# Latent stage in one block: norm, turn, queries, keys and values tile by tile, with all split weights on chip

## Chip, cores and metric

The kernel runs on one core of one Trainium2 chip. The metric is the time of one execution in microseconds (us), the median of several runs. A core has TensorE (PE), VectorE (DVE), ScalarE (ACT), GpSimd (POOL), and SyncE (SP), which here only issues transfers; sixteen DMA engines move data. Engines run their own instruction lists and meet through semaphores.

## What is computed

Two blocks of two layers each work on x, 1024 tokens by 1024. The change concerns the first layer of the second block, an attention over 1024 "latent" tokens whose keys and values come from the latents and from 256 context tokens:

```python
h  = modulate(rmsnorm_2(x, g_pre_mix[i]), shift_m, scale_m)
hc = modulate(rmsnorm_2(ctx, g_pre_mix[i]), cshift_m, cscale_m)
q, k, v = qkv_proj(h, w_qkv[j], g_q[j], g_k[j])      # 8 query heads, 2 key heads of 128
q = apply_axial_rope(q, cos, sin)
k = apply_axial_rope(k, cos, sin)
kc, vc = kv_proj(hc, w_qkv[j], g_k[j])               # context: keys and values only
k_all, v_all = concatenate([kc, k]), concatenate([vc, v])
y = latent_attention(q, k_all, v_all) @ w_o[j]
x = x + gate_m * rmsnorm_2(y, g_post_mix[i])
```

`w_qkv` is 1024 by 1536. Keys are normalised per head and multiplied by a gain; those of the latents are also rotated.

## The kernel before

Tokens stand in tiles of 128 on the partitions: 8 latent tiles in `X` and 2 context tiles. Each product is done three times, since both operands are split into a high part and what it leaves ("low"): high by high, high by low, low by high. The weights of `w_qkv` are three chunks of 512 columns (0 and 1 are queries, 2 is keys and values), each of 8 slices of 128 rows (`KT` is 8), so a tile's chunk takes 24 matmuls of 512 columns.

The stage runs in blocks one after another, and between two blocks all engines meet at a barrier:

1. `keep_rows` makes six row vectors for later stages and stores them.
2. `copies` loads the context rows; `gained` makes the pre-norm gains.
3. `turn` for the 2 context tiles: squares (ACT, L488), 1/sqrt (POOL), scaled rows (DVE, L511), eight PE transposes a tile (L615), columns times gain (DVE), plus shift (POOL), high part (ACT, L553), low part (DVE, L601).
4. `project` for chunk 2 of the context. POOL splits the weights slice by slice (high L243, low L246) into a ring of 4. The loop runs over chunks, slices and, innermost, tiles; each tile has its PSUM bank, and the banks are drained after each chunk by DVE (L402) and ACT (L417).
5. `gained`, `turn` and `project` again for the 8 latent tiles and all 3 chunks: 576 matmuls.
6. `copies` loads the rotation tables and the gains of queries and keys.
7. `heads` twice: norm, gain and rotation of the keys; then `turn_keys`: their transposes (PE L1388), high (ACT L1401) and low parts (DVE L1413).
8. `latent_attention`, then `turn` and `project` with `w_o`, as blocks of their own, and from there one long block that begins with `Residual`.

Queries go to `q_rows`, a second buffer of 32 KB a partition; `X` keeps the old rows, and `Residual` adds the two. Before the second mixer `X` had also been stored to DRAM as `x_kept`, and it is read back in `mixer_out`.

SP issues all transfers in one queue (q1).

## Time and profile before

| | |
|---|---|
| median of 3 runs (3928.38 to 3941.7) | 3938.45 us |
| the profiled execution | 3941.49 us |
| its span, first to last instruction | 3939.7 us |
| PE busy | 3501.0 us (89%) |
| DVE, ACT, POOL busy | 2223.2, 1653.0, 1414.8 us |
| mean granted TensorE clock | 0.931 |

The span is what the trace covers; some 1.8 us of the execution lie outside it. Of the clock, 1.00 is 2.4 GHz and 0.50 is 1.2 GHz. Times within the trace count from the first instruction. A row in order of time has the start, the duration, the engine, the line, what is written and read, and in brackets how long the engine had been idle and who released it. Matmul ends are modelled, so the distance between two starts says more than a duration.

### The profile page before, as it was taken

Reading aid. Unit: us, or ns where it says so; the run is one execution under the profiler, and the core shown is the slowest. Engines: PE = TensorE matmul, PEld = TensorE weight load, DVE = VectorE, ACT = ScalarE, POOL = GpSimd, SP = SyncE. Lnnn points to the kernel's source line nnn. Section 1 sums busy time; section 2 is a strip of 40 time slices with the busy share of each in tenths; the row PEclk is TensorE's granted clock in tenths of the full one; section 3 lists DMA queues with packets and bytes.
Section 4 is the critical chain, followed back from the end, with each engine's and each line's share of the span. In section 5 each row is a group of like instructions: output and inputs, shape, how many; then the busy total and the mean of one; then the engine's idle time right before and its main releaser. Section 6 shows DMA issues by size and latency. Waiting matters only on the chain. (4 is left out here: it accounts for less than half of the span.)

```text
span 3939.7 us, 60153 instructions
## 1 busy us (share of the span) xinstructions
PE 3501.0 (89%) x19010; PEld 3080.6 (78%) x19010; DVE 2223.2 (56%) x4510; ACT 1653.0 (42%) x3892; POOL 1414.8 (36%) x1824
## 2 busy tenths in 40 slices
PE   5999979999999997693999775999999959999998
PEld 4899767999999986582888654888787747888786
DVE  5466766555777773205777437656535556556434
ACT  1277411767777750102343133333324363333333
POOL 2365322555667753522111124444201214444000
PEclk8999979999999988796999887999999779999999
DMA  4311445111222231100000111222345212222354
GB/s 153 110 40 39 176 162 224 57 41 45 61 68 65 67 129 78 43 22 12 1 0 0 40 55 49 80 80 80 107 155 179 67 48 75 80 80 84 126 192 147
DMA packets 95294, 326.69 MB, mean 83 GB/s; under 512 B 10465, under 2 KB 37393, under 8 KB 82322
## 3 DMA queue, kind: packets, MB, share of 16 engines
q1 hardware_dynamic: 95122, 324.61, 23.4%
q8 instruction: 82, 1.34, 0.1%
q14 instruction: 90, 0.74, 0.1%
HBM read 267.66 MB, written 56.91 MB: 82 GB/s over the span
## 5 line engine op out<-in xcount | busy, mean ns | idle before, releaser
L363 PE MATMUL ps<-w_hi,hT_hi 128*128 128x512 f32 x848 | 338.4, 399 | 41.8 <-DVEq L379 25.6
L364 PE MATMUL ps<-w_lo,hT_hi 128*128 128x512 f32 x848 | 336.6, 397 | 0.0
L365 PE MATMUL ps<-w_hi,hT_lo 128*128 128x512 f32 x848 | 336.2, 396 | 0.0
L2098 PE MATMUL ps<-down_high,hidden_high 128*128 128x512 f32 x704 | 277.1, 394 | 15.6 <-DVE hidden_low L1999 15.2
L2081 PE MATMUL ps<-columns_combined,up_high_even 128*128 128x512 f32 x616 | 243.9, 396 | 46.9 <-POOL up_low_even L1866 32.7
L2100 PE MATMUL ps<-down_high,hidden_low 128*128 128x512 f32 x704 | 275.6, 391 | 0.0
L2099 PE MATMUL ps<-down_low,hidden_high 128*128 128x512 f32 x704 | 275.5, 391 | 0.0
L1997 DVE TENSOR_TENSOR down_low<-down_raw,down_high 128x1024 fp32r<-128x1024 f32 x88 | 107.8, 1225 | 272.8 <-ACT down_high L1914 272.8
L2082 PE MATMUL ps<-columns_combined,up_high_even 128*128 128x512 f32 x616 | 243.1, 395 | 0.0
L2083 PE MATMUL ps<-columns_combined,up_low_even 128*128 128x512 f32 x616 | 242.8, 394 | 0.0
L2081 PE MATMUL ps<-columns_combined,up_high_odd 128*128 128x512 f32 x616 | 239.6, 389 | 0.0
L2082 PE MATMUL ps<-columns_combined,up_high_odd 128*128 128x512 f32 x616 | 239.6, 389 | 0.0
L2083 PE MATMUL ps<-columns_combined,up_low_odd 128*128 128x512 f32 x616 | 239.6, 389 | 0.0
L1165 ACT ACTIVATE masked_then_probs<-masked_then_probs,unit_rows 128x256 f32<-128x256 f32 (+1 forms) x512 | 229.1, 451 | 3.2 <-DVE sink_term L1252 1.8
L363 PEld LDWEIGHTS ps<-w_hi,hT_hi 128*128 128x128 f32 x848 | 163.7, 193 | 79.1 <-POOL w_lo L246 13.8
L1914 ACT ACTIVATE down_high<-down_raw 128x1024 fp32r<-128x1024 f32 x88 | 93.1, 1058 | 269.9 <-PE ps L2100 255.5
L1047 PE MATMUL ps<-w_units,hT_hi 128*128 128x384 f32 (+1 forms) x512 | 184.9, 361 | 19.2 <-DVE w_units L1211 12.7
L1102 PEld LDWEIGHTS ps<-v_tiles,probsT 128*128 128x128 f32 x1600 | 200.1, 195 | 1.4 <-issue 1.4
L1049 PE MATMUL ps<-w_units,hT_lo 128*128 128x384 f32 (+1 forms) x576 | 199.4, 346 | 0.0
L1102 PE MATMUL ps<-v_tiles,probsT 128*128 128x64 f32 x1600 | 196.6, 274 | 0.8 <-DVE unit_rows L1325 0.8
L365 PEld LDWEIGHTS ps<-w_hi,hT_lo 128*128 128x128 f32 x848 | 163.2, 193 | 34.8
L364 PEld LDWEIGHTS ps<-w_lo,hT_hi 128*128 128x128 f32 x848 | 163.7, 193 | 34.1
(336 smaller groups left out, 9568.2 us busy)
## 6 DMA issues: line engine op xcount, KB each, us to landing
mod_weights<-in_w_mod SPq DMA_DIRECT2D x24, 2048.0 KB, 8.8
up_raw<-in_w_up SPq DMA_DIRECT2D x44, 1024.0 KB, 4.9
down_raw<-in_w_down SPq DMA_DIRECT2D x88, 512.0 KB, 3.6
hidden_columns<-hidden SPq DMA_DIRECT2D x44, 512.0 KB, 2.6
hidden_columns<-hidden_columns SPq DMA_DIRECT2D x88, 256.0 KB, 3.9
w_raw<-in_w_in_b SPq DMA_DIRECT2D x24, 768.0 KB, 4.5
group_rows<-unit_rows SPq DMA_DIRECT2D x64, 132.0 KB, 1.8
unit_rows<-group_rows SPq DMA_DIRECT2D x64, 132.0 KB, 2.1
```

The costliest lines, as they stand in the source:

```text
L363: nc.tensor.matmul(out, a, w_hi[:, s], start=(k == 0), stop=False)
L364: nc.tensor.matmul(out, a, w_lo[:, s], start=False, stop=False)
L365: last = nc.tensor.matmul(out, b, w_hi[:, s], start=False, stop=(k == KT - 1))
L1049: last = nc.tensor.matmul(zbank, lo, weights(w_hi, a.unit, k), start=False, stop=(k == KT - 1))
L1102: last = nc.tensor.matmul(o_bank[:, h * HD:(h + 1) * HD], pT[:, a.par, h, c], vs[:, tile], start=(c == a.slots[0]), stop=(c == a.slots[-1]))
L1165: act.activation(x, x, ACT.Exp, bias=own, scale=-1.0, accum_out=total).then_inc(core.probs.sem, 1)
L2081: nc.tensor.matmul(out, a_hi, combined.moving(0, z, k), start=(start and k == 0), stop=False, **again)
L2082: nc.tensor.matmul(out, a_hi, combined.moving(1, z, k), start=False, stop=False, **again)
L2083: last = nc.tensor.matmul(out, a_lo, combined.moving(0, z, k), start=False, stop=(k == 3), **again)
L2098: nc.tensor.matmul(out, h_hi[:, s, t], down_hi[:, s, cols], start=begin, stop=False)
L2099: nc.tensor.matmul(out, h_hi[:, s, t], down_lo[:, s, cols], start=False, stop=False)
L2100: last = nc.tensor.matmul(out, h_lo[:, s, t], down_hi[:, s, cols], start=False, stop=end)
```

## The change

Steps 1 to 7 become one block with one phase, `Latents`. It walks 13 slots (`SLOTS`). In slot i every engine does its part for several tiles at once: tile i is normalised and turned to columns, the products of tile i-1 are made, and the keys of tile i-1 are normalised and rotated; keys of tile i-3 are transposed and split. Tiles 0 and 1 are the context (chunk 2 alone), 2 to 9 the latents (chunks 2, 0, 1). All 24 weight slices are split once, high by ACT and low by DVE (chunk 2) or POOL (chunks 0, 1), and stay in SBUF (`qkv_high`, `qkv_low`); slices are loaded in pairs, 12 loads of 512 KB into two buffers, and slots 0 to 3 split four each of slices 8 to 23. The loop over slices is now inside the tile, so 24 matmuls in a row go to one bank. The shift is added where the columns leave PSUM, half by ACT and half by DVE. The row vectors are made in slots 1 and 2. Queries are written over the rows of `X`, which have been stored to `x_kept` (4096 KB) behind the fifth load of weights; `q_rows` is gone, and `Residual` loads the old rows from `x_kept` tile by tile. `heads`, `turn_keys` and `keep_rows` are gone; `latent_attention` itself is the same.

```diff
@@ -2121,12 +1987,13 @@
...
+        self.old = at("residual_old_rows", [P, TILES, D], F32, offset=top)
...
     def sync(self, sp):
         core = self.core
         sp.dma_start(self.factor[:], self.factor_row.partition_broadcast(P)).then_inc(core.post_row.sem, 16)
-        self.combined.load(sp, self.ahead.w_up, 0)
+        for m in range(TILES):
+            sp.dma_start(self.old[:, m], self.kept[:, m]).then_inc((core.ready0, core.ready1)[m % 2].sem, 16)
+            if m == 3:
+                self.combined.load(sp, self.ahead.w_up, 0)
+            if m % 2:
+                sp.wait_ge(core.ready0.sem, core.ready0.at(8 * m + 8))
+                sp.wait_ge(core.ready1.sem, core.ready1.at(8 * m + 8))
...
+                y, ready = X[:, m], (core.ready0, core.ready1)[m % 2]
                 dve.wait_ge(core.y_rstd.sem, core.y_rstd.at(m + 1))
                 dve.scalar_tensor_tensor(y, y, rs[:, 0, m:m + 1], self.factor[:], ALU.mult, ALU.mult).then_inc(core.y_scaled.sem, 1)
                 dve.wait_ge(core.y_scaled.sem, core.y_scaled.at(m + 1))
-                dve.tensor_tensor(X[:, m], X[:, m], y, ALU.add).then_inc(core.x_new.sem, 1)
+                dve.wait_ge(ready.sem, ready.at(8 * (m - m % 2) + 16))
+                dve.tensor_tensor(y, y, self.old[:, m], ALU.add).then_inc(core.x_new.sem, 1)
...
+class Latents:
...
+    SLOTS = ALL_TILES + 3
...
+        self.w_hi = core.sb(st, "qkv_high", [P, 3, KT, 512], F32R)
+        self.w_lo = core.sb(st, "qkv_low", [P, 3, KT, 512], F32R)
+        self.raw = core.sb(st, "qkv_raw", [P, 2, 2, 512])
+        self.T_hi = core.sb(st, "columns_high", [P, 2, KT, P], F32R)
+        self.T_lo = core.sb(st, "columns_low", [P, 2, KT, P], F32R)
...
+    def sync(self, sp):
+        core = self.core
+        sp.dma_start(self.C[:], self.ctx_rows).then_inc(core.loads.sem, 16)
+        def load(p):
+            c, k = self.slice_at(2 * p)
+            sp.dma_start(self.raw[:, p % 2], self.w[c][:, k:k + 2]).then_inc((core.raw0, core.raw1)[p % 2].sem, 16)
+        load(0)
+        load(1)
...
+        for p in range(2, 3 * KT // 2):
+            if p < 2 + KT // 2:
+                sp.wait_ge(core.split.sem, core.split.at(2 * p - 2))
+            else:
+                sp.wait_ge(core.up_lo.sem, core.up_lo.at(2 * p - 2 - KT))
+            load(p)
+            if p == 4:
+                sp.dma_start(self.kept, self.X[:]).then_inc(core.x_kept.sem, 16)
+        sp.wait_ge(core.links_act.sem, core.links_act.at(1))
+        sp.dma_start(self.lines_dram.rearrange("n (k p) -> (n k) p", p=P), self.lines[:]).then_inc(core.row_vectors.sem, 16)
+        sp.wait_ge(core.row_vectors.sem, core.row_vectors.at(16))
...
+    def gpsimd(self, pool):
...
+        def low(n):
+            c, k = self.slice_at(n)
+            pool.wait_ge(core.high.sem, core.high.at(n + 1))
+            pool.nop(nofuse=True)
...
+        for i in range(self.SLOTS):
+            t = self.tile(i + 1)
+            if t is not None:
+                rstd(t)
+            if i < 4:
+                for n in range(KT + 4 * i, KT + 4 * i + 4):
+                    low(n)
...
+    def scalar(self, act):
...
+        def high(n):
+            c, k = self.slice_at(n)
+            if n % 2 == 0:
+                raw = (core.raw0, core.raw1)[(n // 2) % 2]
+                act.wait_ge(raw.sem, raw.at(16 * (n // 4) + 16))
+            act.activation(self.w_hi[:, c, k], self.raw[:, (n // 2) % 2, n % 2], ACT.Copy).then_inc(core.high.sem, 1)
+        square(0)
+        for n in range(4):
+            high(n)
+        square(1)
+        for i in range(self.SLOTS):
+            t = self.tile(i + 1)
...
+                square(t)
+            t = self.tile(i)
+            if t is not None:
...
+                for k in range(4):
+                    act.activation(self.tmp[:, k], ps[:, 0, k * P:(k + 1) * P], ACT.Identity, scale=self.pre[:, self.of(t), k:k + 1],
+                                   bias=self.shifts[self.of(t)][:, k:k + 1]).then_inc(core.n_columns.sem, 1)
+                act.wait_ge(core.n_columns.sem, core.n_columns.at(4 * t + 4))
+                act.wait_ge(core.n_columns_dve.sem, core.n_columns_dve.at(4 * t + 4))
+                if t >= 2:
+                    act.wait_ge(core.products.sem, core.products.at(t - 1))
+                    if t >= 2 + CTX_TILES:
+                        act.wait_ge(core.val.sem, core.val.at(t - 1 - CTX_TILES))
+                act.activation(self.T_hi[:, t % 2], self.tmp[:], ACT.Copy).then_inc(core.hi_done.sem, 1)
...
+            if i < 4:
+                for n in range(KT + 4 * i, KT + 4 * i + 4):
+                    high(n)
+            t = self.tile(i - 1)
+            if t is not None:
+                act.wait_ge(core.products.sem, core.products.at(t + 1))
+                if t >= 2:
+                    act.wait_ge(core.kq_turned.sem, core.kq_turned.at(t - 1))
+                act.activation(self.k_rows[:, t % 2], ps[:, 4 + t % 2, 0:KV2 * HD2], ACT.Copy).then_inc(core.parts_act.sem, 1)
+                act.activation(self.v[:, t], ps[:, 4 + t % 2, KV2 * HD2:], ACT.Copy).then_inc(core.parts_act.sem, 1)
+                act.wait_ge(core.parts_act.sem, core.parts_act.at(2 * t + 1))
...
+                act.activation(self.k_sq[:], self.k_rows[:, t % 2], ACT.Square).then_inc(core.sq.sem, 1)
...
+                    act.wait_ge(core.val.sem, core.val.at(m + 1))
+                    if m == 0:
+                        act.wait_ge(core.x_kept.sem, core.x_kept.at(16))
+                    act.activation(self.X[:, m, 512:D], ps[:, 7, :], ACT.Copy).then_inc(core.acc_used_act.sem, 1)
...
+                act.wait_ge(core.kq_turned.sem, core.kq_turned.at(t + 1))
+                act.activation(self.kT_hi[:, :, t * P:(t + 1) * P], ps[:, 2 + t % 2, 0:KV2 * P].rearrange("p (g t) -> p g t", t=P), ACT.Copy)\
+                   .then_inc(core.kq_hi.sem, 1)
...
+    def vector(self, dve):
...
+                if t + 1 < ALL_TILES:
+                    normed(t + 1)
+                dve.wait_ge(core.hi_done.sem, core.hi_done.at(t + 1))
+                dve.tensor_tensor(self.T_lo[:, t % 2], self.tmp[:], self.T_hi[:, t % 2].bitcast(F32), ALU.subtract).then_inc(core.lo_done.sem, 1)
...
+            t = self.tile(i - 1)
+            if t is not None:
+                k3 = self.k_rows[:, t % 2].rearrange("p (h d) -> p h d", d=HD2)
+                sq3 = self.k_sq[:].rearrange("p (h d) -> p h d", d=HD2)
+                dve.wait_ge(core.sq.sem, core.sq.at(t + 1))
+                dve.reduce_sum(self.ksum[:, t], sq3, axis=AX_X).then_inc(core.sums.sem, 1)
+                if t >= CTX_TILES:
...
+                        dve.wait_ge(core.x_kept.sem, core.x_kept.at(16))
+                    dve.tensor_copy(self.X[:, m, 0:512], ps[:, 6, :]).then_inc(core.acc_used_dve.sem, 1)
+                dve.wait_ge(core.rstd.sem, core.rstd.at(t + 1))
...
+    def tensor(self, pe):
...
+        def product(t, c, bank, done):
+            for k in range(KT):
...
+                a, b = self.T_hi[:, t % 2, k], self.T_lo[:, t % 2, k]
+                nc.tensor.matmul(ps[:, bank, :], a, self.w_hi[:, c, k], start=(k == 0), stop=False)
+                nc.tensor.matmul(ps[:, bank, :], a, self.w_lo[:, c, k], start=False, stop=False)
+                last = nc.tensor.matmul(ps[:, bank, :], b, self.w_hi[:, c, k], start=False, stop=(k == KT - 1))
+            last.then_inc(done.sem, 1)
+        for i in range(self.SLOTS):
...
+                for k in range(KT):
+                    last = nc.tensor.transpose(ps[:, k // 4, (k % 4) * P:(k % 4 + 1) * P], self.nrows[:, k * P:(k + 1) * P], core.ident[:])
+                last.then_inc(core.n_turned.sem, 1)
+            t = self.tile(i - 1)
+            if t is not None:
+                pe.wait_ge(core.lo_done.sem, core.lo_done.at(t + 1))
+                if t >= 2:
+                    pe.wait_ge(core.parts_act.sem, core.parts_act.at(2 * t - 2))
+                product(t, 2, 4 + t % 2, core.products)
+                if t >= CTX_TILES:
+                    m = t - CTX_TILES
+                    if m >= 1:
+                        pe.wait_ge(core.acc_used_dve.sem, core.acc_used_dve.at(m))
+                    product(t, 0, 6, core.gate)
+                    if m >= 1:
+                        pe.wait_ge(core.acc_used_act.sem, core.acc_used_act.at(m))
+                    product(t, 1, 7, core.val)
...
+                for g in range(KV2):
+                    last = nc.tensor.transpose(ps[:, 2 + t % 2, g * P:(g + 1) * P], self.k_rows[:, t % 2, g * HD2:(g + 1) * HD2], core.ident[:])
+                last.then_inc(core.kq_turned.sem, 1)
...
-        keep_rows()
...
-                T = split_columns(st2)
...
-                    C = q_rows[:, 0:CTX_TILES]
-                    copies(core, [(C, I["ctx"][0].rearrange("(m p) n -> p m n", p=P))])
...
-                    turn(core, CTX_TILES, Stage(core, x_rows(C)), T, scale=pre[:], shift=mod_ctx[:, 0:8],
-                         ahead=weights)
-                    project(core, T, plain_tokens, CTX_TILES, weights, 1, lambda m, c: kv_rows[:, m])
-                gained(core, pre[:], vcol("g_pre_mix"), mod[0][:, 8:16])
-                weights = Weights(core, st2, I["w_qkv"])
-                turn(core, TILES, Stage(core, x_rows(X)), T, scale=pre[:], shift=mod[0][:, 0:8], ahead=weights)
-                project(core, T, plain_tokens, TILES, weights, 3, lambda m, c: (
-                    kv_rows[:, CTX_TILES + m] if isinstance(c, int) else q_rows[:, m, bass.ds(c * 512, 512)]))
+                latents = Latents(core, st2, X, x_dram, I["ctx"][0].rearrange("(m p) n -> p m n", p=P), I["w_qkv"], I["gain_k2"], tables,
+                                  I["axial"], (kT_hi, kT_lo), v, RowVectors(core, vcol, mod, pre_ffn), rows_dram,
+                                  (mod_ctx[:, 8:16], mod[0][:, 8:16]), (mod_ctx[:, 0:8], mod[0][:, 0:8]))
+                in_one_block(core, [latents])
...
-                copies(core, [(tables[:], I["axial"]), (gain_q[:], I["gain_q2"].partition_broadcast(P)),
-                              (gain_k[:], I["gain_k2"].partition_broadcast(P))])
...
-                heads(core, CTX_TILES, keys, KV2, HD2, gain_k[:])
-                heads(core, TILES, lambda m: keys(m + CTX_TILES), KV2, HD2, gain_k[:], rotated)
-                turn_keys(core, keys, kT_hi, kT_lo)
-                latent_attention(core, tile_part(q_rows)(0, D), gain_q[:], tables, kT_hi, kT_lo, kv_rows[:, :, KV2 * HD2:], top)
...
+                copies(core, [(gain_q[:], I["gain_q2"].partition_broadcast(P))])
+                latent_attention(core, tile_part(X)(0, D), gain_q[:], tables, kT_hi, kT_lo, v)
+        with ExitStack() as st:
+            T = split_columns(st)
+            weights = Weights(core, st, I["w_o"])
+            turn(core, TILES, Rows(core, tile_part(X)(0, D)), T, ahead=weights)
+            project(core, T, plain_tokens, TILES, weights, 2, lambda m, c: X[:, m, bass.ds(c * 512, 512)])
```

Three places in the order of instructions. First the transfers that SP issues. Before, from the row vectors to the last load ahead of attention (`w_raw` are the weights, `q_rows` holds the context rows here):

```order
L3133 DMA row_vectors<-row_lines 48x128 [waits links_dve]
L3106 UNCONDITIONAL_BRANCH [waits row_vectors]
L2403 UNCONDITIONAL_BRANCH [waits barrier_Pool_Activation_PE_DVE_SP_release]
L2406 DMA q_rows<-in_ctx 128x2x1024
L2402 UNCONDITIONAL_BRANCH [waits loads]
L619 UNCONDITIONAL_BRANCH [waits barrier_Pool_Activation_PE_DVE_SP_release]
L233 DMA w_raw<-in_w_qkv 128x2048 x2
```

Now, the whole block and the load ahead of attention:

```order
L2459 DMA context_rows<-in_ctx 128x2x1024
L2463 DMA qkv_raw<-in_w_qkv 128x1024 x2
L2466 DMA gain_keys<-in_gain_k 128x256
L2467 DMA axial<-in_axial 128x1024
L2463 DMA qkv_raw<-in_w_qkv 128x1024 [waits split] x3
L2475 DMA x_kept<-x 128x8192
L2463 DMA qkv_raw<-in_w_qkv 128x1024 [waits split]
L2463 DMA qkv_raw<-in_w_qkv 128x1024 [waits up_lo] x6
L2477 DMA row_vectors<-row_lines 48x128 [waits links_act]
L3210 UNCONDITIONAL_BRANCH [waits row_vectors]
L2278 UNCONDITIONAL_BRANCH [waits barrier_Pool_Activation_PE_DVE_SP_release]
L2281 DMA gain_queries<-in_gain_q 128x1024
```

The store of `x` has moved between the fifth and the sixth load of weights, and each later load waits until a buffer has been split.

Second, ScalarE. Before, in the turn of the latent tiles it did nothing but squares and high parts:

```order
L488 ACTIVATE squares,sum_sq<-q_rows 128x1024 [waits rstd] x2
L553 ACTIVATE hT_hi<-columns 128x8x128 [waits shifted] x2
L544 REGISTER_ALU
L544 COMPARE_AND_BRANCH
L533 UNCONDITIONAL_BRANCH
```

Now, from slice 8 in slot 0 to the columns of tile 1 in slot 1 (`qkv_raw` are the loaded slices):

```order
L2540 ACTIVATE qkv_high<-qkv_raw 128x512 [waits raw0]
L2540 ACTIVATE qkv_high<-qkv_raw 128x512
L2540 ACTIVATE qkv_high<-qkv_raw 128x512 [waits raw1]
L2540 ACTIVATE qkv_high<-qkv_raw 128x512
L2531 ACTIVATE squares,statistics<-x 128x1024 [waits y_squared]
L2533 ACTIVATE statistics<-statistics,eps 128x1 [waits y_squared]
L2557 ACTIVATE columns<-ps,modulation_ctx,pre_gains 128x128 [waits lo_done,n_turned]
```

The splits of weights stand in ScalarE's list ahead of the columns of the next tile, and wait there for their loads.

Third, TensorE. Before, the transposes of the keys stood in a block of their own, behind all products:

```order
L365 MATMUL ps<-w_hi,hT_lo 128x512
L299 UNCONDITIONAL_BRANCH
L1380 UNCONDITIONAL_BRANCH [waits barrier_Pool_Activation_PE_DVE_SP_release]
L1382 UNCONDITIONAL_BRANCH
L1382 ISA
L1386 REGISTER_ALU [waits staged]
L1388 MATMUL ps<-identity,key_rows 128x128 [waits lo_done]
```

Now, from the end of slot 3 to the first product of slot 4 (`normed_rows` is the next tile):

```order
L2691 MATMUL ps<-qkv_high,columns_low 128x512
L2732 MATMUL ps<-identity,key_rows 128x128 [waits staged]
L2732 MATMUL ps<-identity,key_rows 128x128
L2700 MATMUL ps<-identity,normed_rows 128x128 [waits n_columns_dve,n_columns,n_rows]
L2700 MATMUL ps<-identity,normed_rows 128x128 x7
L2689 MATMUL ps<-qkv_high,columns_high 128x512 [waits parts_act,lo_done]
L2690 MATMUL ps<-qkv_low,columns_high 128x512
```

Key transposes and the turn of the next tile now stand between the products of two tiles.

## Rows read from the trace of the kernel before

**Rows 1.** Busy time by stretch: PE, PEld, DVE, ACT, POOL, then PEclk, DMA, GB/s.

```profile
1541.00:1571.00 30.00, 4.13 (x18) 3.47 (x18) 8.98 (x22) 4.30 (x6) 14.54 (x14) 0.56 0.30 106
...
1584.00:1637.00 53.00, 14.46 (x65) 12.99 (x64) 28.95 (x35) 17.48 (x25) 36.33 (x32) 0.64 0.11 40
1637.00:1771.00 134.00, 133.34 (x576) 110.03 (x576) 8.03 (x12) 6.58 (x11) 37.99 (x40) 0.98 0.09 32
1771.00:1830.00 59.00, 5.78 (x22) 3.52 (x20) 25.05 (x65) 11.98 (x31) 20.32 (x44) 0.52 0.06 20
```

**Rows 2.** VectorE in order of time: stage start, first drain of two chunks.

```profile
1540.88 0.17 DVE L3109 TENSOR_TENSOR row_columns<-vectors,modulation 128x8 f32<-128x8 f32 x1 [0.31 <-PEq L299]
...
1679.58 0.69 DVE L402 COPY q_rows<-ps 128x512 f32 x1 [44.02 <-PE ps L365]
...
1723.09 0.69 DVE L402 COPY q_rows<-ps 128x512 f32 x1 [38.75 <-PE ps L365]
```

**Rows 3.** ScalarE in order of time: last drain, after the loads, latent attention, residual.

```profile
1771.26 0.60 ACT L417 ACTIVATE kv_rows<-ps 128x512 f32<-128x512 f32 x1 [0.76 <-PE ps L365]
1777.94 0.72 ACT L682 ACTIVATE head_squares<-kv_rows 128x256 f32<-128x256 f32 x2 [6.08 <-DVEq L711]
...
1830.31 1.06 ACT L1590 ACTIVATE query_squares<-q_rows 128x1024 f32<-128x1024 f32 x1 [0.89 <-PEq L1379]
...
2341.48 1.49 ACT L2210 ACTIVATE residual_columns_even<-ps,modulation,pre_gain_ffn 128x128 f32<-128x128 f32 x4
```

**Rows 4.** TensorE in order of time: products after idling, and ten transposes.

```profile
1571.51 0.63 PE L364 MATMUL ps<-w_lo,hT_hi 128*128 128x512 f32 x1
1571.94 0.63 PE L365 MATMUL ps<-w_hi,hT_lo 128*128 128x512 f32 x1
...
1576.43 0.39 PE L363 MATMUL ps<-w_hi,hT_hi 128*128 128x512 f32 x1
1576.66 0.39 PE L364 MATMUL ps<-w_lo,hT_hi 128*128 128x512 f32 x1
...
1855.54 1.25 PE L1509 MATMUL ps<-identity,probs 128*128 128x128 f32 x10
```

**Rows 5.** DMA issues between 1454.5 and 1456 us: KB each, us to landing.

```profile
x<-x_kept SPq DMA_DIRECT2D x1, 4096.0 KB, 14.0
w_raw<-in_w_out_b SPq DMA_DIRECT2D x1, 1024.0 KB, 16.0
```

**Rows 6.** DMA issues of the whole page, KB each, median us to landing.

```profile
down_raw<-in_w_down SPq DMA_DIRECT2D x88, 512.0 KB, 3.6
...
w_raw<-in_w_qkv SPq DMA_DIRECT2D x8, 1024.0 KB, 4.9
```

**Rows 7.** Groups by line, 1540 to 1831 us: busy, mean ns, idle before.

```profile
L246 POOL TENSOR_TENSOR w_lo<-w_raw,w_hi 128x512 fp32r<-128x512 f32 x27 | 34.7, 1286 | 4.2 <-POOL w_hi L243 0.4
...
L553 ACT ACTIVATE hT_hi<-columns 128x1024 f32 (+1 forms) x10 | 10.6, 1057 | 37.9 <-POOL columns L567 37.9
...
L488 ACT ACTIVATE squares<-x 128x1024 f32 x8 | 8.3, 1043 | 1.2 <-PEq L2521 1.2
...
L511 DVE TENSOR_SCALAR rows<-x,rstd 128x1024 f32 x8 | 6.0, 754 | 11.9 <-POOL rstd L503 11.9
...
L682 ACT ACTIVATE head_squares<-kv_rows 128x256 f32 (+1 forms) x10 | 3.9, 413 | 32.1 <-DVE kv_rows L727 21.7 <-DVEq L711 10.4
```

**Rows 8.** VectorE in order of time, 2400 to 2412 us: the same subtraction twice.

```profile
2401.80 2.72 DVE L1738 TENSOR_TENSOR residual_columns_odd<-residual_columns_odd 128x512 f32<-128x512 f32 x1
...
2411.20 0.69 DVE L1744 TENSOR_TENSOR residual_columns_odd<-residual_columns_odd 128x512 f32<-128x512 f32 x1
```

**Rows 9.** GpSimd in order of time, the same stretch.

```profile
2401.40 2.58 POOL L1866 TENSOR_TENSOR up_low_even<-up_raw,up_high_even 128x1024 fp32r<-128x1024 f32 x1 [2.45 <-ACT up_high_even L1901]
```

**Rows 10.** The chain that ended last, start of the residual phase.

```profile
2325.88 4.29 DMA residual_factor<-row_vectors
...
2331.52 1.24 DVE x L2266
```

385 lines of the change are left out of this document (213 added, 172 removed).

## The prediction, made before the changed kernel had run

> **What bounds the stage now.** I read the busy time by stretch first, since the totals of the page mix stages. The stage begins with VectorE's first row vector at 1540.9 us [rows 2] and ends where latent attention begins on ScalarE, at 1830.3 [rows 3]: 289.4 us. Only one of its stretches is full. From 1637 to 1771 TensorE is busy 133.3 of 134 us, at a granted clock of 0.98 [rows 1]. Everywhere else it mostly waits: in 1541 to 1571 it works 4.1 us of 30, in the turn of the latent tiles (1584 to 1637) 14.5 of 53, while the keys are finished (1771 to 1830) 5.8 of 59 [rows 1]. So some 155 us of the stage hold next to no products, and the reader is to see that no other engine fills them either: they are chains through several engines with barriers between. What the change can give is at most what lies outside the products.
>
> **The floor.** VectorE drains the first two chunks 43.4 us apart (1679.58 and 1723.09) [rows 2]. That is 192 matmuls, 0.2264 us each, as the distance between two starts at full clock shows too (0.23) [rows 4]. The same matmuls stay: 48 for the context and 576 for the latents, 141.3 us. Transposes cost 0.115 us each at full clock (ten take 1.25 with the tail of the last) [rows 4], so a tile's eight take about 1.0.
>
> **A full slot (tiles 3 to 9).** Eight transposes 1.0, 72 matmuls 16.3, two key transposes 0.3, hand-overs 0.1: 17.7 us. Does TensorE wait within it? ScalarE may take the keys of tile i-1 only when the key transposes at the end of slot i are done (the buffer `k_rows` has two places), so its work bunches behind each slot. From there to a free bank for chunk 0: ScalarE's two copies and a square of 256 columns, 0.41 each [rows 7], a VectorE sum of about the same, VectorE's drain 0.69 [rows 2], with hand-overs about 3 us. TensorE meanwhile has 1.0 of transposes and 5.4 of chunk 2. The columns of the next tile follow: its square 1.04 [rows 7], the mean, four columns 1.49 [rows 3], high part 1.06 [rows 7], low part 1.3 to 1.6, in all about 8 us after the slot's end, and needed only after 17.7. Nothing waits. What hides the keys is thus the 16.3 us of products; without it they would cost what they cost now, most of the 59 us from 1771 on [rows 1] over ten tiles, 5 us a tile.
>
> **The ramp (slots 0 to 3).** Zero is the block's start. The context rows are issued at 0.3 and land in 4.9, as the other 1024 KB load does [rows 6]. Square, 1/sqrt, scaling (0.75) [rows 7], eight transposes at half clock (TensorE has idled; 2 us), ScalarE's first four splits and second square, columns, high and low part: the first low part is done at about 15.7, and the context product of tile 0 fits between 16 and 24. The loads of slices 4 to 7, 3.6 us each [rows 6], arrive at 13 to 15. The fifth load waits for six low parts, which VectorE has at 17.3; the store of `x` (4096 KB) goes out right behind it at 17.8, and the sixth load at 18.8. In the trace a 4096 KB transfer lands in 14.0, and a 1024 KB load issued just behind it in 16.0 [rows 5], where one alone takes 4.9 [rows 6]: one queue, served in order. The sixth load is half that size, so I take 15.2: it lands at 34. ScalarE stands at slice 10 until then, with the square of tile 2 and the columns of tile 1 behind it in its list.
>
> After 34: two splits 1.2 (about 0.6 for 512 columns, half of the 1.06 for 1024), square and mean 1.5, columns 1.5, high 1.1, low 1.3, and 0.4 of hand-overs: the product of tile 1 starts at 41. It runs at half clock for its first 4 us (starts 0.43 apart) and then at full clock (0.23) [rows 4]: 7.4 us, to 49. The low parts of slices 12 to 15 keep GpSimd until 46 (1.29 each) [rows 7]; only then does it make the 1/sqrt for the keys of tile 0, and VectorE has that ahead of tile 2's columns. So tile 2 is ready at 52. From there TensorE is not idle again: chunks 2, 0 and 1 of tile 2 take 16.3 us, to 68.4. Slices 20 to 23 are loaded by 60, high by 63 and low by 66.5; chunk 1 wants its last slice at 67.7. That is close, 1.2 us.
>
> **One correction to the ramp.** GpSimd's subtractions run beside VectorE's here. VectorE's subtraction of two 512-column operands takes 0.69 us alone and 2.72 [rows 8] where GpSimd has a 2.58 us subtraction under way [rows 9]: VectorE waits for that operation to end. In slots 1 to 3 eleven small operations for the row vectors and about six larger ones meet sixteen such GpSimd operations of 1.29. If each of the seven small two-operand ones waited once, that is 9 us; if none did, nothing. I take 1.5, near the lower end, since VectorE has no other work until GpSimd is through at 46. The Trainium skill, "SBUF — State Buffer", section "Who interferes with whom", says the same of the pair of ports that the two engines share: an exclusive lock for the whole instruction. By that rule, if all seven meetings lay on the path, the sum would be 3862; it is the part of the skill that speaks against this change.
>
> **Sum.** Slot 3 ends at 68.4 + 0.3 + 1.5 = 70.2. Seven full slots add 123.9: 194.1. The tail (last drain, two rounds of key transposes, high and low parts) is 3.5, the barrier 0.3: 198. The block that loads the query gain stays: from the last drain to the next ScalarE work it takes 6.1 us with three loads now (1771.9 to 1777.9) [rows 3], and 5.3 with one. The stage lasts 203.2 us in place of 289.4, a gain of 86.2.
>
> **Residual.** VectorE added the first row of y at 2331.5, 5.6 us after the factor was issued at 2325.9 [rows 10]. Now the old row (512 KB) comes behind the factor (512 KB) in the queue. The two are as large as one 1024 KB load, 4.9 us [rows 6], which with two issues and a hand-over is 5.6, the moment of today's addition; two separate loads of 3.6 in a row would be 7.9. I take 1.1 us later, nearer to the first; the chain of the phase starts with that addition, so it is lost in full (bounds 0 and 2.5). The later rows are issued in pairs well before their turn. `latent_attention` and the `w_o` stage do the same work as now, on other addresses: 0. They start at half clock as now, since TensorE idles in front of them either way.
>
> 3941.5 - 86.2 + 1.1 = 3856 for the profiled execution, which is 3 us above the median of the three runs; against that median the forecast is 3854.
>
> **Rivals.**
> 1. The store of `x` does not hold up the sixth load. Against it stand the 16.0 us [rows 5]. For it: that load was behind a read, this one is behind a write. The sixth load would then land at 24 and not at 34, less what the buffers then cost: 3845.
> 2. The weights set the pace of the ramp: the loads take longer than 3.6 us beside each other, or the lock above costs more. Each of six loads from the seventh on can add 1 to 2 us once chunk 1's 1.2 us of slack is used: 3862 to 3870.
> 3. The full slots are longer, because the bunched work of ScalarE and VectorE takes more than the 6.4 us that I give it before chunk 0. At 3 us a slot that is 21: 3875. For it: every hand-over in the list of ScalarE is in order and I counted 0.1 each. Against it: the margin is twice the chain. In this case too the key work is not hidden, and the change does only half of what it says.
> 4. Slower than before: TensorE is granted half clock in the full slots. With starts 0.43 apart [rows 4], a slot is 33 us; from six of eight such slots on the change loses, and with all eight the time is 3854 + 8 x 15.5 = 3978. Against it: the clock is 0.98 over 134 us of the same products [rows 1]; for it only that in each slot the engine does short transposes and waits on more semaphores.
>
> **Chances.** Forecast 0.62, rival 1 0.12, rival 2 0.15, rival 3 0.08, rival 4 0.02, and 0.01 for no net change from several small causes. The range 3838 to 3872 takes in the forecast with an error of some 10 us in a ramp worked out, rival 1 and rival 2, and leaves out rivals 3 and 4. A measurement of this kernel tells a change from none at about 0.3%, 12 us. Faster by more than that 0.97, within it 0.01, slower 0.02.
>
> **What would show it.** In the trace after: one stretch of some 140 us with TensorE over 97% busy and a clock near 1.00; full slots 17.7 us apart (look at the first transpose of each tile); ScalarE idle for more than 10 us in slot 0, released by a transfer into `qkv_raw`; tile 2's first product 52 to 54 us after the block's start; latent attention beginning 203 us after it; in the residual phase a first addition released by `residual_old_rows`. The forecast is wrong if a slot is longer than 18.5 us, if chunk 1 of tile 2 waits for `qkv_low` for several us, if the ScalarE wait is missing, or if attention itself takes another time.

## The result

| | before | after |
|---|---|---|
| median of the runs, us | 3939.6 (3928.4 to 3941.7, 4 runs) | 3849.4 (3843.0 to 3852.0, 4 runs) |
| ratio, 95% interval | | 0.9774 (0.9752 to 0.9796) |
| profiled execution: span | 3939.7 | 3848.0 |
| latent stage, block start to latent attention | 289.4 | 201.5 |

The forecast was 3854, range 3838 to 3872. The two spans differ by 91.7 us. Along the trace this is made up of: a stage that starts 1.0 earlier (same code ahead of it), the stage itself 87.9, latent attention and the `w_o` stage 0.1 (495.6 us from the first query square to the issue of the residual factor before, 495.5 after), the residual phase -0.2 (from that issue to the first store of hidden columns 114.0 before, 114.2 after), and 2.8 in the unchanged rest. The thirteen profiles of this study, the kernel before among them, ran that rest in 1492 to 1500 us, so the 2.8 can't be told from chance.

Busy time by stretch of the changed kernel, with the columns of [rows 1]: ramp to the sixth weight load, tile 1, tile 2, the seven full slots, the tail with the block that loads the query gain.

```profile
1539.80:1571.00 31.20, 11.04 (x40) 8.64 (x40) 10.59 (x23) 11.02 (x22) 3.60 (x4) 0.62 0.82 305
1571.00:1588.60 17.60, 10.46 (x41) 8.33 (x41) 11.55 (x23) 12.89 (x28) 10.39 (x11) 0.69 0.30 94
1588.60:1608.20 19.60, 19.47 (x74) 15.78 (x75) 4.71 (x11) 7.61 (x17) 11.83 (x11) 0.84 0.18 56
1608.20:1729.70 121.50, 121.50 (x571) 101.25 (x568) 40.85 (x91) 33.44 (x80) 19.07 (x40) 1.00 0.00 1
1729.70:1741.30 11.60, 0.86 (x4) 0.29 (x2) 4.00 (x10) 2.38 (x7) 2.34 (x5) 0.72 0.14 45
```

TensorE is busy through all of the fourth stretch, at full clock. The keys' 59 us of [rows 1] have shrunk to the last row. Of what TensorE waits for in the stage, the view of waits leaves three lines:

```profile
PE ps L2700 <- DVE normed_rows L2607: 27.2, 4, 14.3
PE ps L2732 <- DVE kT_lo L2676: 5.5, 1, 5.5
PE ps L2689 <- DVE columns_low L2636: 0.6, 1, 0.6
```

ScalarE in order of time: the splits of slices 8 and 10, the high part of tile 2, a key copy behind each of slots 3 and 4 and behind the last full one, the start of latent attention.

```profile
1560.02 1.15 ACT L2540 ACTIVATE qkv_high<-qkv_raw 128x512 fp32r<-128x512 f32 x2 [3.76 <-DMA qkv_raw<-in_w_qkv]
1570.95 1.15 ACT L2540 ACTIVATE qkv_high<-qkv_raw 128x512 fp32r<-128x512 f32 x2 [9.79 <-DMA qkv_raw<-in_w_qkv]
...
1586.36 1.06 ACT L2565 ACTIVATE columns_high<-columns 128x1024 fp32r<-128x1024 f32 x1 [3.62 <-issue]
...
1608.52 0.38 ACT L2577 ACTIVATE key_rows<-ps 128x256 f32<-128x256 f32 x1 [8.44 <-PE ps L2732]
...
1626.24 0.38 ACT L2577 ACTIVATE key_rows<-ps 128x256 f32<-128x256 f32 x1 [9.70 <-PE ps L2732]
...
1729.78 0.38 ACT L2577 ACTIVATE key_rows<-ps 128x256 f32<-128x256 f32 x1 [14.86 <-PE ps L2732]
...
1741.33 1.06 ACT L1456 ACTIVATE query_squares<-x 128x1024 f32<-128x1024 f32 x1 [4.89 <-PEq L2277]
```

The second row is the wait behind the store of `x`. In a full slot ScalarE idles 9.4 to 9.7 us, for the key transposes: that is the spare time which the products leave it.

VectorE in slot 1: a normalised tile, the row vectors, the sum for the keys of tile 0, their scaling, and only then tile 2's columns.

```profile
1574.76 0.75 DVE L2607 TENSOR_SCALAR normed_rows<-x,statistics 128x1024 f32<-128x1024 f32 x1 [16.41 <-POOL statistics L2486]
...
1577.13 1.23 DVE L2758 TENSOR_TENSOR row_columns<-vectors,modulation 128x8 f32<-128x8 f32 x1
...
1582.46 0.41 DVE L2650 TENSOR_REDUCE statistics<-key_squares 128x2 f32<-128x256 f32 x1
1584.11 0.43 DVE L2658 TENSOR_TENSOR key_squares<-key_rows,statistics 128x256 f32<-128x256 f32 x1 [1.24 <-POOL statistics L2509]
...
1584.92 1.36 DVE L2631 TENSOR_SCALAR columns<-ps,pre_gains,modulation 128x128 f32<-128x128 f32 x4
```

GpSimd over the same time, four weight subtractions in one row, and the first step of the keys' 1/sqrt:

```profile
1576.61 5.47 POOL L2492 TENSOR_TENSOR qkv_low<-qkv_raw,qkv_high 128x512 fp32r<-128x512 f32 x4 [1.89 <-ACT qkv_high L2540]
1583.04 0.19 POOL L2506 TENSOR_SCALAR statistics<-statistics 128x2 f32<-128x2 f32 x1 [0.95 <-DVE statistics L2650]
```

GpSimd is through with its subtractions and then waits 0.95 us for VectorE's sum of the keys.

TensorE at tile 2: the turn of tile 3 after a pause, then products 0.43 apart (half clock), and from 1594.85 on 0.23 apart.

```profile
1587.00 1.09 PE L2700 MATMUL ps<-identity,normed_rows 128*128 128x128 f32 x8 [2.07 <-DVE normed_rows L2607]
1588.73 0.79 PE L2689 MATMUL ps<-qkv_high,columns_high 128*128 128x512 f32 x1 [0.64 <-DVE columns_low L2636]
1589.33 0.63 PE L2690 MATMUL ps<-qkv_low,columns_high 128*128 128x512 f32 x1
...
1594.85 0.40 PE L2691 MATMUL ps<-qkv_high,columns_low 128*128 128x512 f32 x1
```

### The profile page after: what moved, and what is told of

It is laid out like the page before. It is cut to its first block and busy times, and to the rows that moved or that the text cites. A ratio compares the mean times of both kernels' runs of the same rounds, so it can differ in the third digit from the quotient of the medians.

```text
span 3848.0 us, 59509 instructions
## 1 busy us (share of the span) xinstructions
PE 3490.4 (91%) x19010; PEld 3071.8 (80%) x19010; DVE 2220.8 (58%) x4533; ACT 1680.2 (44%) x3971; POOL 1344.5 (35%) x1756
## 5 line engine op out<-in xcount | busy, mean ns | idle before, releaser
L363 PE MATMUL ps<-w_hi,hT_hi 128*128 128x512 f32 x640 | 254.9, 398 | 21.3 <-ACTq L410 9.1
L364 PE MATMUL ps<-w_lo,hT_hi 128*128 128x512 f32 x640 | 253.8, 397 | 0.0
L365 PE MATMUL ps<-w_hi,hT_lo 128*128 128x512 f32 x640 | 253.5, 396 | 0.0
L1157 DVE CUSTOM_DVE_ANT_0 masked_then_probs<-ps,mask 128x256 f32<-128x256 f32 (+1 forms) x512 | 156.2, 359 | 59.4 <-PE ps L978 59.0
L2362 DVE SCALAR_TENSOR_TENSOR mod_sums<-mod_weights,silu_c,mod_sums 128x512 f32 x196 | 183.7, 949 | 6.0
L961 PE MATMUL ps<-w_units,hT_hi_by_fours 128*128 128x384 f32 (+1 forms) x512 | 183.6, 359 | 0.0
```

The costliest lines, as they stand in the source:

```text
L363: nc.tensor.matmul(out, a, w_hi[:, s], start=(k == 0), stop=False)
L364: nc.tensor.matmul(out, a, w_lo[:, s], start=False, stop=False)
L365: last = nc.tensor.matmul(out, b, w_hi[:, s], start=False, stop=(k == KT - 1))
L961: nc.tensor.matmul(zbank, hi, weights(w_hi, a.unit, k), start=(k == 0), stop=False)
```

## Experiments

Two questions: what holds the ramp (the store of `x`, the shared port, the clock), and how well the products cover the rest. In the table, times count from the issue of the context rows; "half" is how many of tile 2's 72 products start 0.4 us apart or more; "rest" runs from the first store of hidden columns to the end, the same code in all. The last four columns are of the one profiled execution. Medians stand beside different medians of the kernel before (3936.7 to 3941.3), so the ratio compares better than the median, and both are too coarse (their intervals are some 6 us to each side) for most of what follows: the stage decides.

| kernel | median | ratio to before (95%) | low part of tile 2 starts | half | stage | rest |
|---|---|---|---|---|---|---|
| the changed kernel | 3849.4 | 0.9774 (0.9752 to 0.9796) | 47.6 | 14 | 201.5 | 1497.0 |
| the same once more | 3850.6 | 0.9767 (0.9751 to 0.9783) | 47.5 | 14 | 201.5 | 1497.0 |
| store late | 3839.4 | 0.9739 (0.9723 to 0.9755) | 38.5 | 3 | 190.3 | 1499.0 |
| store on ScalarE's queue | 3849.0 | 0.9771 (0.9755 to 0.9787) | 46.8 | 4 | 198.9 | 1491.8 |
| the same in pieces | 3842.7 | 0.9753 (0.9737 to 0.9769) | 42.5 | 6 | 194.8 | 1496.6 |
| row vectors early | 3847.2 | 0.9764 (0.9747 to 0.9780) | 47.3 | 0 | 198.4 | 1496.9 |
| filled pause | 3846.7 | 0.9764 (0.9748 to 0.9781) | 47.5 | 0 | 198.6 | 1500.2 |
| late + early | 3832.4 | 0.9738 (0.9721 to 0.9754) | 37.5 | 0 | 188.5 | 1492.1 |
| late + early + filled | 3838.3 | 0.9748 (0.9732 to 0.9764) | 38.8 | 0 | 190.0 | 1496.9 |
| late + early + 1/sqrt sooner | 3837.5 | 0.9738 (0.9722 to 0.9754) | 37.6 | 0 | 188.5 | 1499.3 |
| up load first (residual) | 3851.4 | 0.9776 (0.9759 to 0.9792) | 47.6 | 2 | 199.2 | 1497.9 |

**1. The store behind the last weight load.**

```
-            if p == 4:
+            if p == 3 * KT // 2 - 1:
                 sp.dma_start(self.kept, self.X[:]).then_inc(core.x_kept.sem, 16)
```

> The store of x (4096 KB) is issued behind the last weight load instead of behind the fifth. Theory A (the queue serves in order, so the store holds up the sixth load, and the sixth load holds the whole ramp, since ScalarE has the square of tile 2 and the columns of tile 1 behind it): the sixth load lands 4 to 5 us after its issue in place of 13.9, every later step of the ramp up to slot 3 moves forward by 8 to 9 us, the latent stage lasts 193 us in place of 201.5, and the kernel takes about 3841. Theory B (the ramp is paced by the weights' own loads, splits and GpSimd subtractions, and the store's wait only hides that): the sixth load lands earlier, but tile 2 starts less than 3 us sooner, because the next loads or subtractions become the wait; 3846 to 3850. Theory C (the store is now late itself: the first overwritten row of x, or the row vectors behind the store in the queue, waits for it): a new wait of several us at the end of slot 3, 3849 or more.

Theory A, with a little more than its number. The sixth load is split at 22.0 us after the start instead of 31.1, the low part of tile 2 begins 9.1 sooner, and the stage is 11.2 shorter (8 to 9 expected); the other 2 us are tile 2's products, which take 17.2 in place of 19.3, see 5 and 6. The late store lands 60.9 us after the start, and no later slot is longer for it (17.45 as before). ScalarE in this kernel, with the columns as above:

```profile
1560.72 1.16 ACT L2540 ACTIVATE qkv_high<-qkv_raw 128x512 fp32r<-128x512 f32 x2 [3.25 <-DMA qkv_raw<-in_w_qkv]
1563.37 1.15 ACT L2540 ACTIVATE qkv_high<-qkv_raw 128x512 fp32r<-128x512 f32 x2 [1.49 <-DMA qkv_raw<-in_w_qkv]
```

**2. The store on a queue of its own.** The line above is taken out of SyncE's list, and ScalarE issues the same transfer between the splits of slices 7 and 8.

> The store of x is issued by ScalarE, on a queue of its own, at nearly the moment at which it was issued before (between the splits of slices 7 and 8), so that it runs beside the sixth load but not ahead of it in its queue. Theory A (order within one queue is what costs): the sixth load lands in at most 8 us, twice its time alone since two transfers share the engines, and the kernel takes 3842 to 3845. Rival (bandwidth: 4096 KB keep the DMA engines full whichever queue they are in): the sixth load takes 10 to 14 us as before, and the kernel 3848 to 3851.

The rival. The fifth load, issued 0.4 us behind the store on the other queue, now takes 12.9 us, where it took 4.7 ahead of it; the sixth takes 12.8 (13.8 before) and is split at 29.8. The transfers of this kernel in its window 1554 to 1560 (q10 is ScalarE's queue, q1 SyncE's; packets, MB, share of 16 engines):

```profile
q10 hardware_dynamic: 72, 2.36, 94.7%
q1 hardware_dynamic: 32, 0.13, 5.3%
```

A packet of the store is 33 KB, one of the weights 4 KB. From 1557.6 to 1564.9, where both queues are at work, they move the same number of packets:

```profile
q10 hardware_dynamic: 80, 2.62, 91.4%
q1 hardware_dynamic: 80, 0.33, 10.9%
```

The Trainium skill, "DMA: Bandwidth & Descriptors", section "Queues, rings and completion order", says that an engine takes turns between queues packet by packet. This trace agrees, 80 to 80. So I asked next whether it is the bytes or the packets.

**3. The same store in pieces.**

```
-                act.dma_start(self.kept, self.X[:]).then_inc(core.x_kept.sem, 16)
+                for m in range(TILES):
+                    act.dma_start(self.kept[:, m], self.X[:, m]).then_inc(core.x_kept.sem, 16)
```

> The store of x on ScalarE's queue again, at the same moment, but as eight transfers of 512 KB, 4 KB for each partition and tile, where the single one moved 32 KB a partition in packets of some 29 KB. Theory A (the two queues take turns by packet, so a weight load with packets of 3.7 KB got about an eighth of the engines beside the large ones): with packets of like size the fifth load, which took 12.8 us beside the single store, lands in 6 to 9 us, and the sixth no later than 24 us after the start of the stage in place of 29.8; stage 193 to 197. Rival (the bytes issued first go first, whatever their packets): fifth load 11 to 13 us, stage 198 to 200. In both, ScalarE spends 2 to 3 us on issuing.

Theory A, with the sixth load 0.9 us later than its bound of 24 (24.9). The fifth load lands in 5.3 us and the sixth in 7.9, and in the window 1554 to 1560 its queue has 29.7% of the engines, with packets of like size on both sides:

```profile
q10 hardware_dynamic: 344, 1.29, 61.0%
q1 hardware_dynamic: 144, 0.52, 29.7%
```

Here the turns are longer than a packet: from 1556.58 to 1557.58 the queue of the weights moved 62 packets and the store none, from 1558.58 to 1559.58 it was 5 against 109. This edit also spreads the store's issues over 9 us, so it does not test the size of packets alone; the equal counts of experiment 2 are the closer evidence. The expected 2 to 3 us of issuing was wrong: ScalarE's eight issues lasted from 1553.6 to 1562.4, 8.7 us, each of the later ones up to 1.6 where a lone one takes 0.34, and after 1554.8 it split nothing until they were through. With that the sixth load was split 3.0 us later than with the late store, out of 4.5 us between the two stages.

**4. The row vectors in slot 0.** The call `self.rows.vector(dve, self.row_cols)` moves from slot 1 to the end of slot 0.

> The eleven small row-vector operations of VectorE move from slot 1, where they take 5 us beside four GpSimd subtractions (1.2 us each instead of 0.16), to slot 0, where VectorE idles for 16 us. Theory A (the prediction's: VectorE has nothing else to do until GpSimd is through, since the 1/sqrt of the keys of tile 0 stands behind those subtractions in GpSimd's list): the stretched operations vanish, but tile 2's columns start only about 1 us sooner, stage 200.5, kernel 3848. Rival (the stretch by the shared port lies on the path): tile 2 is ready 4 to 5 us sooner, TensorE then has no gap and no half clock before it, stage 195 to 197, kernel 3842 to 3845.

Each small operation now takes 0.16 us, and the eleven together 0.9 in place of 5.3, yet the low part of tile 2 starts only 0.3 sooner. But this run was 0.5 us late at the split of slice 10 already, since its first loads landed later; from the split of slice 10 to that low part it takes 15.6 us in place of 16.5. The two kernels with the store late differ by the same 0.9 (15.6 and 16.5). That is theory A on the waits: of the 4.4 us of stretch 0.9 lay on the path, the wait of GpSimd for VectorE's sum. But the stage is 3.1 shorter, more than A gave, and the rest is in tile 2's products, 16.5 us in place of 19.3: TensorE's pause ahead of the turn of tile 3 is 1.39 us in place of 2.07, and all 72 products of tile 2 run at full clock. TensorE in this kernel:

```profile
1588.43 1.09 PE L2699 MATMUL ps<-identity,normed_rows 128*128 128x128 f32 x8 [1.39 <-DVE normed_rows L2607]
1590.17 0.50 PE L2688 MATMUL ps<-qkv_high,columns_high 128*128 128x512 f32 x1 [0.64 <-DVE columns_low L2636]
```

**5. The pause filled.**

```
+            if i == 3:
+                for _ in range(12):
+                    nc.tensor.matmul(ps[:, 2, :], self.w_hi[:, 2, 0, 0:P], self.w_hi[:, 2, 1], start=True, stop=True)
```

> The changed kernel with twelve matmuls more, into a bank that nobody reads, between the product of tile 1 and the transposes of tile 3, where TensorE idles for 2.1 us now. Theory A (tile 2's first fourteen matmuls run at half clock because of that pause, which costs 0.2 us each, 2.8 us): tile 2's products start at the same moment as before, all 0.23 apart, and last 16.4 us in place of 19.3; stage 198.5 to 199.5, kernel 3846 to 3847. Rival (the half clock comes from the longer idle time ahead of tile 1, or the added matmuls delay the transposes): tile 2's products still take 19 us or start later; stage 201 to 203, kernel 3849 to 3851.

Theory A: tile 2's first product comes 48.8 us after the start, where it came at 48.9, and the 72 take 16.5 us in place of 19.3.

**6. The changed kernel once more.**

> The changed kernel once more, unaltered, to see what one and the same code varies by. Theory A (the clock of tile 2's products behind the short pause is chance, since the residual experiment, whose latent stage is unaltered too, had 2 of them at half clock and the changed kernel 14): some number between 0 and 14 matmuls at half clock, stage 198.5 to 201.5 with the rest of the ramp within 0.3 us of the changed kernel's, kernel 3845 to 3851. Rival (14 is what this kernel does, and the residual experiment differed by something upstream): 12 to 14 at half clock, stage 201 to 202.

The rival, as far as this run goes. Over all kernels the pattern is this: where TensorE paused 1.8 to 2.8 us ahead of the turn of tile 3 (seven profiles, counting the shortened products of 9), some products of tile 2 ran at half clock, 2 to 14 of them; where the pause was 1.6 or less or was filled (five), none. In the profiles with 2 to 4 the transposes themselves were already slow (1.6 to 2.0 us for eight in place of 1.09), so the clock fell earlier and was back earlier. What decides when it falls is not settled, and since the pauses differ by other changes too, their length is a pattern and not a shown cause; shown is that filling the pause took the half clock away (5). It makes 2.3 us of difference between the stage of the residual kernel and this one, whose latent stage is the same code.

**7. Two and three at once.** Late store and early row vectors:

> Store of x behind the last weight load, and the row vectors' operations in slot 0, together. Theory A (two causes in a row: the ramp is 11.2 us shorter by the first alone and 3.1 by the second alone, but the second gains most by the clock of tile 2's products, of which the first has some already): stage 188 to 190 against 201.5 of the changed kernel and 190.3 with the store alone; kernel 3837 to 3839. Rival (with the store gone, the small operations are themselves what holds the ramp): they add their full 3 us or more, stage 187 or less, kernel 3835 or less.

Theory A: 188.5. Its median, 17 us under the changed kernel's and in the rival's reach, flatters it: its rest ran in 1492.1, and the kernel before ran in 3936.7 beside it, 2.9 less than beside the changed kernel. The stage says 13.0. The ratio is that of the late store alone (0.9738 and 0.9739): only the stages tell the two apart. With the twelve matmuls as well:

> Store late, row vectors early, and the twelve matmuls more. Theory A (clock and waits each give what they give alone, less what the first two leave over): 0 to 1.5 us less than with the first two alone, stage 187 to 189. Rival (the added matmuls now run into the transposes of tile 3, which have less of a pause ahead of them): stage 1 to 2 us longer than with the first two alone.

The rival in its mechanism, not in its price. The twelve matmuls last 2.8 us, longer than the pause of 1.6, and the turn of tile 3 starts 1.2 us after its rows are ready. But most of the 1.5 us that the stage is longer has another source: this run was 1.1 us late from its first load on, and 1.35 at the split of slice 10. Net of that the filling costs 0.2 us.

**8. The keys' 1/sqrt one subtraction sooner.** On top of late and early, in slots 1 and 2:

```
-                for n in range(KT + 4 * i, KT + 4 * i + 4):
+                for n in range(KT + 4 * i, KT + 4 * i + (3 if i in (1, 2) else 4)):
                     low(n)
...
                 pool.tensor_tensor(krs, krs, core.minus_half[:, 0:KV2], ALU.pow).then_inc(core.rstd.sem, 1)
+                if i < 3:
+                    low(KT + 4 * i + 3)
```

> Store late and row vectors early, and in slots 1 and 2 GpSimd makes the 1/sqrt of the keys one weight subtraction earlier (three subtractions, the 1/sqrt, the fourth). Theory A (behind the first two causes the ramp hangs on that 1/sqrt, since VectorE has it ahead of tile 2's columns): the low part of tile 2 starts 36 to 36.5 us after the start of the stage in place of 37.5, the stage lasts 187 to 187.7 in place of 188.5, kernel 3830 to 3838, which times alone can't tell from the version with two changes. Rival (the fourth subtraction is then late for the slices of chunk 0 or chunk 1, or ScalarE is late with the squares of the keys): no gain, stage 188 to 189.5.

No gain, but for neither reason of the rival. GpSimd starts its fourth subtraction 0.07 us before VectorE's scaling of the keys, and that then takes 1.51 us in place of 0.43. GpSimd, then VectorE:

```profile
1569.82 1.30 POOL L2492 TENSOR_TENSOR qkv_low<-qkv_raw,qkv_high 128x512 fp32r<-128x512 f32 x1
```

```profile
1569.89 1.51 DVE L2659 TENSOR_TENSOR key_squares<-key_rows,statistics 128x256 f32<-128x256 f32 x1 [1.26 <-POOL statistics L2509]
```

The scaling starts 1.0 us sooner than with late and early alone, and ends no sooner: here the shared port costs 1.1 us on the path. (The run was also 0.25 late at the split of slice 10, so 0.2 may have been gained.)

**9. How much the products cover.** All chunks of the eight latent tiles are cut to their first slice:

```
-            for k in range(KT):
+            KS = KT if t < CTX_TILES else 1
+            for k in range(KS):
```

> The products of the eight latent tiles are cut to their first slice in all three chunks (9 matmuls a tile in place of 72), so that TensorE needs only about 3.5 us a slot; its time is not the reference's, only the length of a slot is looked at. Theory A (the other engines' chain behind each slot is about 8 us, well under the 17.4 of a full slot, so queries, norms and keys are hidden): slots of 8 to 10 us. Rival (the chain through the keys and the two-place buffer is nearly as long as a slot, and the full slots are only just covered): 14 us or more.

Theory A: ScalarE takes the key rows every 7.96 us in the last slots, and there it never idles for them. (This kernel leaves out seven eighths of the latent tiles' products; its one execution took 3776.5 us, and its stage 127.7.) What is left of a slot still has a turn and nine products, in part at half clock: from 1617.66 to 1625.62 the granted clock is 0.83. So 7.96 is the most that the side work needs from one tile to the next. It is not the length of the chain behind one slot, which runs on into the next.

```profile
1617.66 0.36 ACT L2577 ACTIVATE key_rows<-ps 128x256 f32<-128x256 f32 x1
...
1625.62 0.37 ACT L2577 ACTIVATE key_rows<-ps 128x256 f32<-128x256 f32 x1
...
1633.58 0.36 ACT L2577 ACTIVATE key_rows<-ps 128x256 f32<-128x256 f32 x1
```

That chain is 9.1 us long in the changed kernel's full slots, from ScalarE's key copy at 1626.24 to the end of the next tile's low part:

```profile
1634.08 1.23 DVE L2636 TENSOR_TENSOR columns_low<-columns,columns_high 128x1024 fp32r<-128x1024 f32 x1 [0.52 <-ACT columns_high L2565]
```

**10. A later first addition.** In the residual phase `self.combined.load(sp, self.ahead.w_up, 0)` moves ahead of the loop over the old rows.

> In the residual phase the first weight load (1024 KB) goes ahead of the old rows in the queue, so that the first addition waits 3 to 4 us longer. Theory A (the prediction's: the chain of the phase starts with that addition, so what it is late is lost in full): the first store of hidden columns comes 117 to 118.5 us after the factor was issued in place of 114.2, kernel 3852 to 3854. Rival (the phase has slack behind its first addition, as the trace of the changed kernel hints, where an addition 0.9 us later left that store 0.2 later): 114 to 115, kernel 3849 to 3850.

Theory A in the stretch of the phase, while the median (3851.4) tells neither theory from the other: the first addition comes 8.9 us after the factor's issue in place of 6.6, the eighth 50.9 in place of 48.6, and the first store of hidden columns 117.2 in place of 114.2. So the 2.3 us are kept in full through all eight rows. In the kernel before the eighth came at 47.6, so the changed kernel too keeps its 1.0 that far. The other 0.7 appears, or is lost, in the 21.4 us ahead of that store, in which TensorE makes the first hidden columns; before, changed, and this kernel, with the columns of [rows 1]:

```profile
2409.68:2431.08 21.40, 14.76 (x54) 12.04 (x55) 10.55 (x10) 6.62 (x7) 8.16 (x4) 0.76 0.15 50
2321.58:2342.98 21.40, 14.82 (x57) 12.14 (x58) 10.48 (x10) 6.97 (x7) 8.87 (x4) 0.83 0.14 50
2322.53:2343.93 21.40, 14.80 (x54) 12.04 (x55) 10.50 (x10) 6.73 (x7) 8.21 (x4) 0.76 0.15 50
```

The granted clock is 0.76, 0.83 and 0.76. From the eighth addition to that store the thirteen profiles took 65.2 to 66.4 us. VectorE, the two operations of the first row:

```profile
2240.02 1.28 DVE L2137 SCALAR_TENSOR_TENSOR x<-x,statistics,residual_factor 128x1024 f32<-128x1024 f32 x1 [5.41 <-DMA residual_factor<-row_vectors]
2244.31 1.23 DVE L2140 TENSOR_TENSOR x<-x,residual_old_rows 128x1024 f32<-128x1024 f32 x1 [3.01 <-DMA residual_old_rows<-x_kept]
```

## Why the prediction held, step by step

- **The full slot: right, 0.3 too long.** 17.7 was given. A slot with a turn took 17.45 us, and the seven to the last key transposes 121.5, the last without a turn. The chain behind a slot was given as about 8 us; it took 9.1 (9), since VectorE's scaling and rotation of the keys, left out of the sum, stand ahead of its columns. Needed only after 17.4 us, it cost nothing. That the slot with most of the products taken away is 7.96 is another quantity, and its nearness to 8 is chance. Rival 3 is ruled out: by estimate from 7.96 and 17.45, the slot would have to lose more than half of its length before the keys showed.
- **The store of `x`: right, 3 us too late.** The sixth load took 13.8 us, not 15.2, and was split at 31.1, not at 34. In the changed kernel the queue is served in order: from 1560.5 to 1567.5, with the sixth load long issued, it moved the store's large packets alone. But order within the queue is not what makes the store dear: on another queue it delayed the weights as much (2), with equal counts of unequal packets. Rival 1 gave 3845 for a store that delays nothing. Late, it gave 3839, since 2 us of clock came on top.
- **The ramp after it: a little too long in waits, and one term missing.** Tile 1's product started at 37.4 (41 given), tile 2's at 48.9 (52 plus 1.5 for the port). "From there TensorE is not idle again" was right, but the term that failed is the clock: 16.3 us was given for tile 2's products, 19.3 measured, because the pause of 2.1 us ahead of the turn of tile 3 was not priced. Slot 3 ended at 68.4, with 70.2 given: errors of -4.6 and +2.8.
- **The shared port: a stretch of 4.4 us seen, 0.9 lost.** Four small operations took 1.2 us each beside GpSimd. The reason given for a low price was the right one in the main: most of the stretch fell where VectorE would have waited for GpSimd's 1/sqrt in any case (4). The value taken, 1.5, was 0.6 too high for the waits; with the small operations early, tile 2's products also took 2.8 less, which was not priced. By the rule in the Trainium skill, "SBUF — State Buffer", section "Who interferes with whom", the sum was to be 3862 if all meetings lay on the path. An operation that starts beside one of GpSimd's ends only as that one is through (8), so the lock that the Trainium skill describes there agrees with the trace; but on the path lay 0.9 us of it in the changed kernel, and 1.1 in 8.
- **Slack of the last slices: right.** TensorE waits for no weights in tile 2; GpSimd's last subtraction ends 64.3 us after the start, with 66.5 given.
- **Tail: 3.5 + 0.3 given, 7.3 measured.** The term counted a drain and two rounds of turns. It left out that the keys of tile 9 go through the whole chain of norm, gain and rotation with nothing above them: the wait of 5.5 us for `kT_lo` in the list of waits. The block with the query gain took 4.2 us (5.3 given), which gave back some.
- **Residual: 0.9 measured, 1.1 given.** The delay is kept in full through the eighth row, here and in 10. Of it 0.2 arrived at the first store of hidden columns, and in 10 the 2.3 arrived as 3.0: the clock of the stretch between, 0.83 here and 0.76 in the other two, makes the difference of 0.7 either way.
- **Rivals 2 and 4: not seen.** From the eighth on the loads took 3.7 to 3.9 us where 3.6 was given, and TensorE waited for no weights; the clock of the full slots was 1.00.
- **A sum and two signs.** The two drains of [rows 2] lie 43.5 us apart, not 43.4, which moves the floor by 0.1. Of the signs named, two were narrowly missed: ScalarE's wait in slot 0 was 9.8 us and not over 10, and tile 2's first product came at 48.9 and not at 52 to 54.

In sum, -1.8 by the end of slot 3, -2.4 in the slots and +2.5 behind them make 201.5 out of the 203.2 given. The terms were off by up to 4.6 us in both directions, and that the stage came out within 1.7 is in part luck. For the profiled executions 85.1 us of gain were forecast in all, and 91.6 came: 1.7 more from the stage, 0.9 from the residual phase, and 3.9 from code ahead of the stage and behind it that the change does not touch.

## What to carry to other kernels

Finish a side product (here the keys) one slot late under the main product, and check the cover by taking most of the main product away: the slot that is left, 8 of 17.4 us, is the most that the side work needs for one tile. Keep a large transfer that nobody waits for yet out of the stretch in which small loads pace the start; another queue alone doesn't separate them, and 11 us lay there. When a pause of TensorE is priced, look at what the products behind it lose by the clock: here a pause of 2 to 2.8 us was followed by a loss of 0.5 to 2.8 us with the same code.

## What was new about the hardware

- A 4096 KB store with 33 KB packets left the weight loads on the other queue 5% of the DMA engines in their first microseconds (12.9 and 12.8 us for 512 KB), the two queues moving 80 packets each in 7.3 us; in 4 KB packets, issued over 9 us, it left 30% (5.3 and 7.9 us).
- Eight transfers issued in a row by one engine while the DMA engines were full cost that engine 8.7 us, not eight times 0.34.
- VectorE operations on 8 columns, a copy and an addition of a constant among them, took 1.2 to 1.3 us beside GpSimd's subtractions of 1.37, and 0.16 alone.
- The unchanged code behind the stage ran in 1492 to 1500 us over thirteen profiles. An effect of 3 us was visible in its own stretch of the trace, and not in the medians.
